# Two constant tables move to another engine's queue, and one gate's weight rows are read in two earlier parts of a two-block transformer kernel

## The reference, cut to what matters

```python
mod = silu(c) @ w_ada + b_ada                  # w_ada: 2048 x 12288
shift1, scale1, gate1, shift2, scale2, gate2 = split(mod, 6)
h = rms_norm(x) * (1 + scale1) + shift1
aq, ak, av, gq, gf, gi, gg = split(h @ w_in)   # w_in: 2048 x 7168
attn = dilated_attention(rope(norm(aq)), rope(norm(ak)), av)
ho = hgrn2(gq, gf, gi)                         # a gated recurrence, 8 heads
mix = concat(rms_norm(attn), rms_norm(ho) * silu(gg)) @ w_out
x = x + gate1 * mix
h2 = rms_norm(x) * (1 + scale2) + shift2
x = x + gate2 * (relu(h2 @ w_ff1) ** 2 @ w_ff2)
```

## Time and profile before

| | us |
|---|---|
| three timed runs: median (lowest to highest) | 2688.37 (2688.21 to 2689.26) |
| the profiled execution's own time | 2683.85 |
| its span, first to last instruction | 2682.1 |
| busy in the span: PE | 2547.7 |
| busy: DVE | 2000.3 |
| busy: ACT | 1273.0 |
| busy: POOL | 278.1 |

### The profile page before, as it was taken

The page is one execution under the profiler, slowest core; times in us unless marked ns, Lnnn a source line. Parts: engine busy times, 40 slices in busy tenths (PEclk is TensorE's granted clock), DMA queues, the critical chain, the costliest instruction groups (busy, mean ns, idle before and its releaser), DMA issues.

```text
span 2682.1 us, 36228 instructions
## 1 busy us (share of the span) xinstructions
PE 2547.7 (95%) x14307; PEld 2220.3 (83%) x14307; DVE 2000.3 (75%) x2232; ACT 1273.0 (47%) x1590; POOL 278.1 (10%) x323
## 2 busy tenths in 40 slices
PE   5999999998999999999989999888899999999998
PEld 4777777777999989998867788767799998999897
DVE  6788858998877888788888677876765566565556
ACT  4544395344454444444445544345445444444443
POOL 0000120202030201001030002451000000020000
PEclk9999999999999999999999999999999999999999
DMA  8998849997888989897965645666567777766664
GB/s 312 316 335 323 275 154 342 322 329 251 298 291 308 319 297 332 267 354 259 329 196 175 180 134 149 196 218 205 192 186 227 226 223 228 226 216 191 190 183 147
DMA packets 298218, 663.88 MB, mean 248 GB/s; under 512 B 20753, under 2 KB 20849, under 8 KB 297025
## 3 DMA queue, kind: packets, MB, share of 16 engines
q1 hardware_dynamic: 294976, 650.21, 72.9%
q0 software_dynamic: 2784, 10.05, 1.1%
q10 hardware_dynamic: 288, 1.31, 0.1%
HBM read 659.39 MB, written 2.10 MB: 247 GB/s over the span
## 4 chain that ended last, share of the span: by engine, by line
PE 75%; DVE 11%; issue 4%; DMA 4%; ACT 4%; POOL 1%; SPq 0%; DVEq 0%; ACTq 0%
PE PS L598 75%; DVE WL L1367 3%; DVE ACC L1375 3%; ACT WH L1000 2%; DMA RAW<-in_w_in 2%; DVE UQ L1367 1%; DMA RAWX<-in_w_ada 1%; DVE hn L1372 1%; PE PS L601 1%; DMA RAW<-in_w_o 0%; ACT L1000 0%; DMA RAWX<-in_w_a_up 0%; DVE acc L1367 0%; ACT UQ L1000 0%; DVE AL L1367 0%
## 5 line engine op out<-in xcount | busy, mean ns | idle before, releaser
L1367 DVE TENSOR_TENSOR WL<-RAW,WH 128x1024 fp32r<-128x1024 f32 x567 | 706.6, 1247 | 404.2 <-ACT WH L1000 403.7
L1000 ACT ACTIVATE WH<-RAW 128x1024 fp32r<-128x1024 f32 x567 | 600.8, 1060 | 831.4 <-PE PS L598 646.4
L598 PE MATMUL PS<-WH,AH 128*128 128x512 f32 x2052 | 815.5, 397 | 25.8 <-DVE WL L1367 12.4
L598 PE MATMUL PS<-WL,AH 128*128 128x512 f32 x2052 | 802.9, 391 | 0.0
L598 PE MATMUL PS<-WH,AL 128*128 128x512 f32 x2052 | 802.7, 391 | 0.0
L598 PE MATMUL PS<-BH,WH 128*128 128x256 f32 x2048 | 583.0, 285 | 5.1 <-DVE BL L1367 5.1
L598 PE MATMUL PS<-BH,WL 128*128 128x256 f32 x2048 | 581.4, 284 | 0.0
L598 PE MATMUL PS<-BL,WH 128*128 128x256 f32 x2048 | 581.4, 284 | 0.0
L598 PEld LDWEIGHTS PS<-WH,AH 128*128 128x128 f32 x2052 | 387.8, 189 | 116.8 <-DVE WL L1367 25.9
L598 PEld LDWEIGHTS PS<-WH,AL 128*128 128x128 f32 x2052 | 387.2, 189 | 82.3
L598 PEld LDWEIGHTS PS<-WL,AH 128*128 128x128 f32 x2052 | 387.7, 189 | 77.7 <-issue 1.0
(11 more groups left out here) (241 smaller groups left out, 2033.3 us busy)
## 6 DMA issues: line engine op xcount, KB each, us to landing
RAW<-in_w_ff SPq DMA_DIRECT2D x335, 512.0 KB, 4.6
RAW<-in_w_ada SPq DMA_DIRECT2D x284, 512.0 KB, 5.1
RAW<-in_w_in SPq DMA_DIRECT2D x192, 512.0 KB, 4.5
RAWX<-in_w_ada SPq DMA_DIRECT2D x100, 512.0 KB, 5.5
RAWY<-in_w_ff SPq DMA_DIRECT2D x96, 512.0 KB, 4.5
RAWX<-in_w_ff SPq DMA_DIRECT2D x81, 512.0 KB, 5.0
RAWX<-in_w_in SPq DMA_DIRECT2D x48, 512.0 KB, 5.3
RAW<-in_w_out SPq DMA_DIRECT2D x32, 512.0 KB, 4.3
```

The source lines that it names most:

```text
L598: return e.matmul(o, l, r, start=start, stop=stop, skip_group_check=True)
L1000: return e.activation(o, i, f, **kw)
L1367: return e.tensor_tensor(o, a, b, op)
```

## The change

Two parts. First, the two DMAs of `CCN` leave POOL's stream and stand in ACT's side work at j = `HG0` + 64 = 539, with the same wait. Second, the 32 items of `gate1` are spread in two parts: the first 16 (rows t = 0 to 7) among chunks 451 to 474, the other 16 among chunks 479 to 529. None is left between 533 and 573. The last one now comes at chunk 529, so the place of `ada_sum` and what follows it is pinned to `OA + 12` = 572, where it was before.

```diff
-    plan += spread(in2, [ada2[2]], 84, 126)
+    plan += spread(spread(in2, [ada2[2][16:]], 30, 84), [ada2[2][:16]], 2, 27)
...
         for b, g in order:
-            tick = st.group_last[b, g][0]
             by_pe = (b, g) == (1, 2)
+            tick = OA + 12 if by_pe else st.group_last[b, g][0]
...
                 for i, s in due(p, HG0, 16, 4, (0, 1, 5, 7)):
                     hgrn(i, s)
+                if j == HG0 + 64:
+
+                    e.wait_ge(s_hm, 48)
+                    e.dma_start(CCN[:, 0:384], C["cc"]).then_inc(s_cc, 16)
+                    e.dma_start(CCN[:, 384:768], C["cn"]).then_inc(s_cc, 16)
...
-
-            e.wait_ge(s_hm, 48)
-            e.dma_start(CCN[:, 0:384], C["cc"]).then_inc(s_cc, 16)
-            e.dma_start(CCN[:, 384:768], C["cn"]).then_inc(s_cc, 16)
             for m in range(4):
```

## The result

| | before | changed |
|---|---|---|
| median of five timed runs, one chip (lowest to highest), us | 2688.21 (2685.56 to 2689.26) | 2678.65 (2673.92 to 2681.42) |
| ratio, 95% interval | | 0.9963 (0.9948 to 0.9977) |
| the profiled execution's own time, us | 2683.85 | 2674.24 |

The changed kernel is 9.6 us faster, 0.37%; the forecast was 14.4 us, and 2674.0. On another chip, later, the same kernel stood at 2673.92 (2672.31 to 2680.01, five runs) against 2688.24 for the one before, 0.9950 (0.9938 to 0.9963): 14.3 us.

What follows compares the result with a forecast made beforehand. PE was taken as the bound in most stretches, with DVE nearly full at 1451 to 1475 and PE waiting at 1688 to 1740. Terms -25.7 + 2.4 + 7.4 + 1.5 = -14.4 us gave 2674.0; range 2665.0 to 2685.0.

Steps and rivals of the forecast that it cites:

- the signs that I had named against myself: PE idle over 12 us at chunks 455 to 478, waits in each recurrence step, or first score waiting for something besides the table.
- Part 1, the table: After chunk 543, PE's wait for the table goes whole, -11.7 us, and the half clock behind it, -1.9.
- rival 4: Tables' DMAs land as late as today, delayed on the DMA side; 1 of 13.6 us stays, net -1.8; chance 0.03.
- rope's last round: POOL's 8 us of steps, awaited by DVE at j = 545, might be late next; priced 0, upper end 5 us.
- Part 2: Rows leaving chunks 533 to 573: -8.2 us in the last recurrence steps, -2.4 at MLO, -1.5 at 1883.08.
- The upper bound of the sum: Upper bound of 29 us on the 25.7 us that goes, if half-clock stretches at 1840 to 1854 go too.
- Part 3, the norm: Up to chunk 455: chunk 452's load waits for a ring slot, +1.9 us; with the rows on DVE, +2.4 together.
- Chunks 461 to 469: DVE is full; six ACC rows cost 7.4 less a 0.9 us lead, 6.5, plus 0.9 for the ring: +7.4 us.
- the ring's part: At chunks 461 to 469, loads need nearer 4.9 than 3.7 us; 0.9 us taken, from 0 to 4.
- From chunk 470 on: DVE idles about 1.5 of each 2.72 us, so an ACC row fits: 0.
- Part 4: 16 rows among chunks 479 to 529: 11 without rope cost 0, 5 with rope 0.3 each, +1.5 us.
- rival 3: Slower: rows at chunks 451 to 529 cost more, sum +15 us, 2704; decided at a mean 0.8 us a row; chance 0.08.

Runs made afterwards that it cites:

- the second profiles: The kernel before and the changed kernel, each unedited and profiled again later: 2690.68 us and 2673.92 us.
- the tables alone: Against the kernel before, only the two CCN DMAs moved to ACT's queue, the 32 gate1 rows left among chunks 533 to 573: 2679.28 us, ratio 0.9969.
- the kernel with the later second part: The changed kernel with its second 16 rows starting at chunk 481 instead of 478: 2676.94 us, one run.
- the short rows: The changed kernel with the 16 gate1 rows of chunks 451 to 474 still loaded but cut to 32 of 1024 columns on VectorE: 2670.17 us, ratio 0.9933.
- the quiet version: The changed kernel with its rows placed instead as 22 among chunks 480 to 515 and 10 among 545 to 559: 2660.69 us, ratio 0.9905.
- the first ones only behind the norm: The changed kernel with its first 16 rows starting at chunk 456 instead of 450, denser up to 474: 2680.63 us, one run.

## Why the prediction was right, and where it was not

**The net effect**, -14.4, is what the traces show (-14.1, and -11.8 between the second profiles), and the range held the time. The runs' median moved by 9.6 on one chip and 14.3 on another. The runs of the kernel before did stand where the forecast took them (2688.21); the weak step was to add the traces' sum to their median: a shift of some us comes with the execution, not with the kernel. That the sum is so close is partly luck. An unforeseen loss of 3.6 at chunks 470 to 477 and 1.0 more with rope than forecast met an unforeseen gain of 3.0 at `MLO` and 0.4 behind it. Of the signs that I had named against myself none came: PE's idle time from chunk 455 to 478 is 8.0 and 8.7 us in the two traces of the changed kernel (12 was the limit), PE waits for `MP` in a few recurrence steps only, and the first score doesn't wait.

**Part 1, the table: right.** -13.5 against -13.6, in full, with the score at full clock. The page of the changed kernel has the DMAs at

```profile
CCN<-const_cc ACTq DMA_DIRECT2D x1, 192.0 KB, 4.0
CCN<-const_cn ACTq DMA_DIRECT2D x1, 192.0 KB, 4.2
```

so the transfer itself took longer than the 3.2 of the earlier trace rows. What was saved is the place behind 8 us of POOL steps (5.9 of them without the rows' part, see the tables alone), and rival 4 fell: the tables alone gave 9.6 to 10.7 us in the traces. The Trainium skill (DMA: Bandwidth & Descriptors, "Issuing engines are not separate DMA queues") says that issuing from other engines saves only the sequencer's time to issue; this case's trace agrees with it for the transfer, and shows what it does not count, what stands ahead of the DMA in the issuing engine's order. Pricing "rope's last round" at 0 with 5 as its upper end was right for this change, and 3.8 for the tables without the rows.

**Part 2: right in mechanism.** The end of the recurrence gave 8.4 (8.2). At `MLO` PE waited 1.66 and 2.75 us before, and a third time behind them:

```profile
1847.57 0.79 PE L598 MATMUL PS<-WH,MHI 128*128 128x512 f32 x1 [2.82 <-DVE MLO L1375]
```

The three waits of the changed kernel on the timeline of PE:

```profile
1833.14 0.41 PE L601 MATMUL PS<-SQ,HG 128*128 128x128 f32 x2 [0.94 <-issue]
...
1834.64 0.73 PE L598 MATMUL PS<-WX,MHI 128*128 128x512 f32 x2 [1.09 <-DVE MLO L1380]
...
1840.95 0.80 PE L598 MATMUL PS<-WH,MHI 128*128 128x512 f32 x1 [2.81 <-DVE MLO L1380]
```

The first two became 2.4 us shorter, just the term. The other 3.0 are the clock: PE's busy time in the windows below falls from 18.77 to 15.77 for the same 72 matmuls. The window of chunks 561 to 564 before (the clock stands behind POOL's column):

```profile
1830.90:1856.90 26.00, 18.77 (x72) 14.88 (x72) 14.21 (x19) 9.84 (x20) 0.00 (x0) 0.80 0.46 151
```

and in the changed kernel:

```profile
1828.20:1848.80 20.60, 15.77 (x72) 12.56 (x72) 9.45 (x15) 9.49 (x20) 0.00 (x0) 0.92 0.32 100
```

0.80 and 0.92 of full clock on average (2.4 GHz; the other level is 1.2): the half level came after both the 2.75 and the 2.82 us pauses before. Now it comes only after the 2.81 us pause; behind the 1.09 us one the granted clock is 1.00. The upper bound of the sum had this ("half-clock stretches at 1840 to 1854 gone too", 29); the value did not.

**Part 3, the norm: right in its mechanism, and within chance in its size.** The prediction had chunk 452's load issued behind the subtraction of chunk 450 and landing 3.7 to 4.0 later, 1.9 in all. The changed kernel, DVE, SP, ACT and PE:

```profile
1415.49 1.22 DVE L1372 TENSOR_TENSOR WX<-RAW,WX 128x1024 fp32r<-128x1024 f32 x1
...
1416.73 1.03 SPq L592 DMA_DIRECT2D RAW<-in_w_in  x2
...
1420.40 1.06 ACT L1000 ACTIVATE WH<-RAW 128x1024 fp32r<-128x1024 f32 x1 [3.81 <-DMA RAW<-in_w_in]
1421.49 1.23 DVE L1372 TENSOR_TENSOR WL<-RAW,WH 128x1024 fp32r<-128x1024 f32 x1 [2.32 <-ACT WH L1000]
...
1424.27 0.73 PE L598 MATMUL PS<-WX,AH 128*128 128x512 f32 x2 [2.16 <-DVE AL L1372]
```

From the slot's end, 1415.49 + 1.22 = 1416.71, to the copy it is 3.7 us; DVE has the chunk 6.0 us after it began chunk 450's subtraction, where it was 4.35 (1411.27 to 1415.62): +1.65. PE's price for the same order goes from 0.8 (chunk 450 at 4.65) to 6.0 (9.86, the kernel with the later second part). What sets the wait was not tried. After waits of 1.16 and 2.16 us (the two traces of the changed kernel) PE goes on at full clock, after 3.94 at half (granted clock 0.50 from 1428.40 to 1431.40). So the forecast's 2.4 is one value of that range, and 1.9 and 0.9 in the two traces of the changed kernel are others. The same product as in the last row, on the timeline of that kernel:

```profile
1428.36 1.22 PE L598 MATMUL PS<-WX,AH 128*128 128x512 f32 x2 [3.94 <-DVE AL L1372]
```

**Chunks 461 to 469: right in size**, 7.2 for 7.4, and the short rows give a split near the forecast's: 5.6 for VectorE (6.5 in the sum) and up to 1.6 for the ring (0.9 in the sum). The reason given for the ring's part, landings nearer 4.9 than 3.7 us, isn't seen: their median is 3.9 from 1459 to 1492 in the changed kernel.

**From chunk 470 on: wrong.** The step that failed is "from chunk 470 on DVE idles about 1.5 of each 2.72 us, an `ACC` row fits: 0". It fits on DVE. But the lead that was lost is made good too slowly there. By lead I mean the time from the end of DVE's subtraction of a chunk to PE's start on it. Before, it is 5.7 us at chunk 472 and 5.8 at 477; in the changed kernel it is 0.1 and 3.2. ACT's copy of chunk 477 in the second profile of before (timeline; in brackets what ended ACT's idle time):

```profile
1496.52 1.06 ACT L1000 ACTIVATE WH<-RAW 128x1024 fp32r<-128x1024 f32 x1 [1.18 <-PE PS L598]
```

and those of chunks 472 and 478 in the changed kernel:

```profile
1494.54 1.06 ACT L1000 ACTIVATE WH<-RAW 128x1024 fp32r<-128x1024 f32 x1 [2.48 <-DMA RAW<-in_w_in]
...
1507.96 1.06 ACT L1000 ACTIVATE WX<-RAW 128x1024 fp32r<-128x1024 f32 x1 [1.57 <-DMA RAW<-in_w_in]
```

Before, the chunk is there, and ACT waits for PE's use of an earlier one; now it waits for the load of each chunk from 471 to 480, because each load starts only when its slot is freed, and lands 4.8 us later (median from 1491 to 1512). The first recurrence step finds the engines so, on the timeline of ACT, DVE and PE in the changed kernel:

```profile
1510.52 1.06 ACT L1000 ACTIVATE WH<-RAW 128x1024 fp32r<-128x1024 f32 x1 [1.50 <-DMA RAW<-in_w_in]
...
1511.41 1.28 DVE L1380 SCALAR_TENSOR_TENSOR ACC<-RAW,CS,ACC 128x1024 f32<-128x1024 f32 x1
...
1511.83 0.50 PE L598 MATMUL PS<-CT,LFH 128*128 128x512 f32 x1 [1.00 <-ACT LFH L1000]
...
1514.08 0.50 PE L598 MATMUL PS<-CT,LFL 128*128 128x512 f32 x1 [1.75 <-DVE LFL L1372]
```

`LFH` stands on ACT behind a copy that waits for its load; `LFL` on DVE behind an `ACC` row and a subtraction; PE pauses 1.00 + 1.75 us and goes on at full clock. In the second profile it pauses 0.96 + 1.75 us and goes on at half clock for some 3 us, which makes the loss 4.8 instead of 3.3. In the kernel with the short rows it goes on at half clock too (granted clock 0.50 from 1508.90 to 1514.00), and a matmul takes 0.63 us and not 0.39:

```profile
1509.52 0.63 PE L598 MATMUL PS<-CT,LFH 128*128 128x512 f32 x1
```

Three runs tell the causes apart. With the same row ahead of 479 and none among chunks 451 to 474 (all rows in the recurrence) chunk 477 takes 4.18, 0.3 more than before: the row alone is nearly free. Without that row and with the first part (5.73) the loss is 1.8. With the first part's loads but not its work on DVE (9.78) it is all there. So it is the lead that was lost to the loads of the first part; the row adds to it. Each of the three is one trace, and the loss differs by 1.6 us between the two traces of the changed kernel, so the shares are rough.

**Part 4: right where there is no rope, low by 1.0 with it.** Eleven rows from 479 to 512 cost 0. The five with rope cost 2.5 and not 1.5, 0.5 each for 0.3; all 32 in the recurrence cost 0.1 each without rope. My own count from the traces is 15.2 us for 32 rows, 0.48 each, against 0.35 forecast and 0.8 for rival 3, which therefore never came near.

**What stays open.** Why a trace's first half differs by up to 7.7 us between executions that do the same was not tried. The losses of 0.8 to 0.9 us in the recurrence came where rows stand ahead of both of two neighbouring chunks with j mod 4 of 2 and 3 (494 and 495, 502 and 503 in the quiet version; 494 and 495, 506 and 507 with all rows in the recurrence, which lost at 493 and 505), and in no kernel where they don't; which of the two rows it is was not taken apart.

## What to carry to other kernels

A small load that sits behind slow steps of its issuing engine costs those steps, not its own transfer; look for an engine that is ahead at that point, and then see what is late next (here rope's last round, worth 3.8 us until the rows left it too). Work that is moved into idle time of an engine also takes a slot and a transfer: price it by the engine's time where the engine is full, and by the lead of the ring where it is not, and don't expect a lead once lost to be back in full before the next step that needs it. Wide VectorE rows beside a chain of small POOL steps lengthen that chain, too. The same 32 rows cost from 2 us (the quiet version) to 19 (the first ones only behind the norm) by where they stand, so the place is worth more experiments than the move.

## What the hardware showed that I had not expected

- Pauses of 1.00 and 1.75 us of PE, one matmul apart, were followed by full clock in one execution (0.39 us a matmul); 0.96 and 1.75 us were followed by half clock in another of the same program (0.63). The same loss became 3.3 or 4.8 us. A wait of 1.84 us with the tables alone was followed by half clock, one of 2.16 us at the norm of the changed kernel by full clock.
- Small POOL steps, 0.2 us long by themselves, mostly took 1.1 to 1.2 us when they met a VectorE row of 1024 columns, and ended with it. The 15 steps of rope's last round took 5.93 us without `ACC` rows, 9.71 with three of them.
- At 291 GB/s, with the DMA engines 87% busy, a ring of four 512 KB slots still kept PE at 25.15 of 26.03 us, in the kernel whose short rows free their slots early.
- The tables' DMAs, 192 KB each, took 4.0 and 4.2 us from ACT's queue beside the weight stream, and 3.2 from POOL's when PE stood still.
